# A third weight lot joins the openings by halves of a 256-token network kernel

## What is computed

```python
def first_block(x, ...):                 # two layers
    for l in range(2):
        h = rms_norm(x, ln1[l]);  x = x + mixer_block(h, ...)
        h = rms_norm(x, ln2[l]);  x = x + swiglu(h, w_ffn_in[l], w_ffn_out[l])

def second_block(x, c, ctx, ...):        # x: 256 tokens, ctx: 256 context tokens
    for layer in range(2):
        x  = x  + 0.5*mx[2]*swiglu_2(modulate(rms_norm_2(x,  g[0]), mx[0], mx[1]), ...)
        xc = xc + 0.5*mc[2]*swiglu_2(modulate(rms_norm_2(xc, g[0]), mc[0], mc[1]), ...)
        hx, hc = modulate(rms_norm_2(x, g[1]), ...), modulate(rms_norm_2(xc, g[1]), ...)
        ox, oc = (mla_mixer, swa_mixer)[layer](hx, hc, ...)
        x = x + mx[5]*ox                 # and then a second feed-forward part;
        ...                              # the context only where it is not the last layer
```

## Time and profile before

| | |
|---|---|
| times of three runs | 2615.62, 2622.36, 2624.57 us (median 2622.36) |
| the profiled execution | 2620.26 us, of which the span of its instructions is 2618.4 us |
| granted clock, mean over the span | 0.997 of full speed |
| PE busy | 2578.4 us, 98% of the span, 14982 matmuls |
| DVE busy | 1725.2 us, 66% |
| ACT busy | 1160.2 us, 44% |
| POOL busy | 39.1 us, 1% |
| read from memory | 399.10 MB |

### The profile page before, as it was taken

The page is one execution under the profiler, slowest core; times in us unless marked ns, Lnnn a source line. Parts: engine busy times, 40 slices in busy tenths (PEclk is TensorE's granted clock), DMA queues, the critical chain, the costliest instruction groups (busy, mean ns, idle before and its releaser), DMA issues.

```text
span 2618.4 us, 37370 instructions
## 1 busy us (share of the span) xinstructions
PE 2578.4 (98%) x14982; PEld 2227.8 (85%) x14982; DVE 1725.2 (66%) x2857; ACT 1160.2 (44%) x1831; POOL 39.1 (1%) x29
## 2 busy tenths in 40 slices
PE   8999999999999999999999999999999999999998
PEld 7999988999998898888887788888888888887887
DVE  6656888765678885677665565556665445576875
ACT  6565555546556552222244542222242222356553
POOL 0000000000000000000000000000000000014000
PEclk9999999999999999999999999999999999999999
DMA  5543577644456664555533024445534445342664
GB/s 192 182 153 128 178 222 218 195 137 153 138 193 202 212 191 145 161 193 179 159 127 101 1 81 149 146 145 156 165 117 145 145 142 176 125 126 65 193 207 140
DMA packets 116860, 404.56 MB, mean 155 GB/s; under 512 B 13264, under 2 KB 18512, under 8 KB 116560
## 3 DMA queue, kind: packets, MB, share of 16 engines
q1 hardware_dynamic: 116688, 402.17, 48.5%
HBM read 399.10 MB, written 1.05 MB: 153 GB/s over the span
## 4 chain that ended last, share of the span: by engine, by line
PE 91%; DVE 5%; ACT 2%; issue 1%; DMA 0%; SPq 0%; DVEq 0%; ACTq 0%
PE psum L645 21%; PE psum L647 21%; PE psum L646 21%; PE psum L651 13%; PE psum L652 6%; PE psum L1087 3%; DVE wlo L1818 1%; ACT whi L1344 1%; DVE arena L1874 1%; DVE HLO L1879 1%; PE psum L1179 1%; PE psum L1151 1%; DMA wring<-w_proj 0%; ACT HHI L1364 0%; PE psum L1169 0%
## 5 line engine op out<-in xcount | busy, mean ns | idle before, releaser
L1818 DVE TENSOR_TENSOR wlo<-wring,whi 128x1024 fp32r<-128x1024 f32 x599 | 725.6, 1223 | 307.6 <-ACT whi L1344 304.7
L1344 ACT ACTIVATE whi<-wring 128x1024 fp32r<-128x1024 f32 x599 | 622.1, 1053 | 397.9 <-PE psum L647 329.7
L645 PE MATMUL psum<-HHI,whi 128*128 128x512 f32 (+1 forms) x1448 | 532.4, 368 | 6.8 <-DVE wlo L1818 3.4
L646 PE MATMUL psum<-HLO,whi 128*128 128x512 f32 (+1 forms) x1448 | 526.5, 364 | 0.0
L647 PE MATMUL psum<-HHI,wlo 128*128 128x512 f32 (+1 forms) x1448 | 526.3, 363 | 0.0
L645 PEld LDWEIGHTS psum<-HHI,whi 128*128 128x128 f32 x1448 | 273.0, 189 | 55.2 <-DVE HLO L1879 5.8
L646 PEld LDWEIGHTS psum<-HLO,whi 128*128 128x128 f32 x1448 | 273.2, 189 | 42.7
L647 PEld LDWEIGHTS psum<-HHI,wlo 128*128 128x128 f32 x1448 | 273.1, 189 | 42.2
L645 PE MATMUL psum<-H,whi 128*128 128x256 f32 x1024 | 298.4, 291 | 8.2 <-DVE wlo L1818 4.3
L646 PE MATMUL psum<-H,whi 128*128 128x256 f32 x1024 | 290.8, 284 | 0.0
L647 PE MATMUL psum<-H,wlo 128*128 128x256 f32 x1024 | 290.7, 284 | 0.0
(11 more groups left out here) (354 smaller groups left out, 3974.2 us busy)
## 6 DMA issues: line engine op xcount, KB each, us to landing
wring<-ffn_in SPq DMA_DIRECT2D x264, 512.0 KB, 4.2
wring<-mod_w SPq DMA_DIRECT2D x144, 512.0 KB, 4.2
wring<-ffn_out SPq DMA_DIRECT2D x96, 448.0 KB, 4.0
wring<-w_proj SPq DMA_DIRECT2D x66, 512.0 KB, 3.8
wring<-w_gate SPq DMA_DIRECT2D x64, 512.0 KB, 4.1
wring<-ffn_out SPq DMA_DIRECT2D x48, 512.0 KB, 3.8
wring<-w_up SPq DMA_DIRECT2D x20, 512.0 KB, 3.5
wring<-w_out SPq DMA_DIRECT2D x16, 512.0 KB, 3.6
```

The source lines that it names most:

```text
L645: mm(out_, w[0], a[0], start=start, stop=False)
L646: mm(out_, w[0], a[1], start=False, stop=False)
L1344: A(whi[:, i % SLOTS, :], wring[:, raw_slot(tag, k), :], ACT.Copy).then_inc(sem("weights_hi"), 1)
L1818: TTN(wlo[:, i, :], wring[:, raw_slot(tag, k), :], whi[:, i, :].bitcast(F32), ALU.subtract).then_inc(sem("weights_lo"), 1)
```

## The change

The third lot (lot 2) is now multiplied in every opening by halves, as it already was in that of `("b0", 0)`. In `half_tail`, ACT converts lot 2 behind the third tile of half 0 and DVE makes its rest there, ahead of the last residual tile of half 1; lot 3 is converted behind all tiles as before. In `qkv` lot 2 is the first query lot. It is multiplied in both halves now, since `open_halves` treats all its lots alike, and the query lots done one by one begin with lot 3.

```diff
             def dense_behind(tag, norm):
-                first = 3 if norm == ("b0", 0) else 2
-                open_halves(tag, [(tag, k) for k in range(first)], norm)
-                for k in range(first, LOTS[tag]):
+                open_halves(tag, [(tag, k) for k in range(3)], norm)
+                for k in range(3, LOTS[tag]):
                     dense_lot(tag, k, BOTH, (HHI, HLO))
...
             def swa_pe():
-                open_halves("qkv", [("sq", j) for j in range(2)], ("b1", 1))
+                open_halves("qkv", [("sq", j) for j in range(3)], ("b1", 1))
...
-                query_lots(range(2, 9))
+                query_lots(range(3, 9))
...
             # ScalarE, half_tail
                 half_hi(norm, 0, range(2, 3), l, n3)
+                split_ahead(tag, lots_[1])
                 act.wait_ge(*done("x_ready", (tag, tiles_[-1])))
...
                 half_hi(norm, 1, range(KT), l, n3)
-                for k in lots_[1:]:
-                    split_ahead(tag, k)
+                split_ahead(tag, lots_[2])
...
             # VectorE, half_tail
                 s(3)
                 r(2)
+                split_ahead(tag, lots_[1])
                 for m in tiles_[:-1]:
                     add_square_half(norm, 1, m)
                 second(tiles_[-1], keys[-1])
...
                 half_norm(norm, 1, l, n3)
-                for k in lots_[1:]:
-                    split_ahead(tag, k)
+                split_ahead(tag, lots_[2])
```

## The result

The changed kernel takes 2626.51 us (median of 20 runs, 2621.1 to 2630.72), the kernel before 2621.27 (20 runs, 2615.62 to 2625.69). The ratio is 1.0018, 95% interval 1.0012 to 1.0024: slower by 4.7 us (3.1 to 6.3). The forecast was 1.1 us faster; the time lies inside the range, and inside 0.3%, but on the other side of nothing. In what follows one execution of 8431 us, of the kernel that leaves out the unread half of `qkv`, stands in that kernel's median (2623.42; 2623.2 without it) and not in its ratio.

The account below looks back on a forecast made before the run. PE was taken as the bound, holding 91% of the last-ending chain. Windows of -0.79, -1.33, -0.80 and +1.80 us (`qkv`) summed to -1.1 us, median 2622.36 to 2621.2 us; range 2615.5 to 2630.

Parts of the forecast that it names:

- The opening's work: Three lots tile by tile in each opening take PE 17.76 us where nothing is missing; waits inside and for lot 2 vanish.
- The head of the opening: PE's new wait for lot 2's rest before its first matmul makes it 1.63 us late, 1.92 in layer 0's second feed-forward.
- The signal term: From DVE's end of lot 2's conversion to PE's start at an opening: 0.03 us added.
- a fall: Granted clock at 0.50 for 3.41 us behind an idle wait of PE; priced at 1.7 us lost each time.
- `qkv`: Its opening also multiplies the context by lot 2, 2.88 us nobody reads; window 19.39 us against 17.59, +1.80.
- rival C: Later waits of PE for DVE in `qkv` swallow the +1.80 us; total -2.9, 2619.4 us; chance 0.10.
- rival B: Row swaps in `qkv` (+3 us) or late first tiles of half 1 (+1.5) are exposed: 2622.8 to 2624.2 us; chance 0.09.
- the favourable end: First tile of half 1 in the openings: about 0.6 us to spare if ACT is free, otherwise nothing.
- rival A: PE's idle 1.5 to 1.8 us at the openings lowers the clock; all four: +5.7 us, 2628.1; chance 0.20.

Follow-up runs that it names:

- the filled version: Changed kernel, but PE does 15 unused matmuls of 256 columns before waiting for lot 2 at the four openings; 2619.47 us, 0.9994 of the kernel before.

## Why the prediction was wrong

**The opening's work: right.** 17.76 us for three lots was taken from the one opening that had them, and 17.77 was measured. The waits for tiles and for lot 2 behind the opening vanished, and PE went on to lot 3 without a wait.

**The head of the opening: the mechanism right, the size too small.** The conversions came out to the hundredth (2.31 us). The signal term did not: 0.03 us, taken from DVE behind ACT, was 0.36 in PE. The fall-free windows are 19.73 to 19.75 us instead of 19.39. That is 0.35 at each of four openings, 1.4 us, and by itself it takes the forecast from -1.1 to about +0.2: the gain was gone without any fall. Against the forecast a fall costs less, 1.50 us and not 1.7, since PE's starts go from 0.12 to 0.21 us apart and not to twice the 0.12.

**`qkv`: right, and a bit dearer.** +1.80 was forecast, +2.15 measured without a fall, and the experiment that leaves the unread half out shows 2.32 us of it in the window. Nothing further on swallowed the loss (rival C): PE's waits behind the scores are 4.1 us against 4.6.

**Tight tiles and swaps (rival B): not seen.** In the changed kernel no wait for a tile or for the swapped queries is among PE's waits. The factor came early enough, since ACT was free, which the text had as the favourable end: in `qkv` ACT is idle for 1.41 us ahead of the factor, and the first tile of the second half is done at 2293.66, where PE needs it near 2294.2.

**The step that failed: the clock (rival A).** The forecast's sum set it to nothing and gave it 2 in 10. Without falls the four windows sum to -0.45 for `down`, about -1.0 for the second feed-forward (19.75 in the filled version, plus the 0.25 by which the unfilled one starts later), -0.46 and +2.15, so to about +0.2 us. Most of the measured +4.7 is the clock: over 20 runs its mean is 0.9955 against the 0.9970 of the kernel before in the later sets. One fall takes half of 3.41 us, 1.7 us, from that mean, and 0.0015 of 2622 us is 3.9, so some 2.3 falls more in a run. At 1.50 us each they cost 3.5 us, which makes +3.7 with the +0.2, inside the interval of +3.1 to +6.3. That PE's idleness brings the falls is shown, not only argued, by the wait filled with idle work: a wait nearly as long, no falls at the openings, the mean clock of the kernel before, 6 us faster.

The text set 0.66 us of idle time, which did nothing, against 2.2 us, which did, placed 1.5 to 1.8 between them and leaned to the harmless side; the missing 0.35 us then brought the idle time to 1.82 and 2.1. It also passed over a third fall in the same trace, behind a stretch of only 1.13 us near the start, where smaller waits break PE's work ahead of it as well:

```profile
27.40 0.39 PE L645 MATMUL psum<-H,whi 128*128 128x256 f32 x1 [1.13 <-DVE wlo L1818]
```

```profile
27.70:31.11 3.41, 3.41 (x18) 3.41 (x17) 3.30 (x6) 1.22 (x2) 0.00 (x0) 0.50 0.56 165
```

The page of the Trainium skill that was weighed there ("TensorE: Matmul & The Clock Gate", section "Why this matters for your kernels") spoke for no fall, and these runs show falls behind idle stretches shorter than it allows for.

**The chance.** Given an idle time between two rows of opposite outcome, the fall deserved at least an even chance at each of four openings, and a single one was enough to decide the sign.

## What to carry to other kernels

A new wait of PE costs its length, less what it saves in waits further on, and, if PE is idle in it, possibly a stretch at half clock behind it; where the trace has no idle time of that size, price both. The remedy is the order of the work: let PE begin with what is ready and join the late operand some steps later, and if there is nothing to do, even useless matmuls were cheaper here than idleness. When a helper takes on one more item, look at what it does to each: only half of what the helper did to the third lot of `qkv` was ever read.

## What the runs showed of the hardware

- **Idle time and the clock.** Over the profiles of these kernels, at the heads of the openings: no fall behind 1.04 to 1.31 us of idle time (four openings), none of three behind 1.71, 8 of 12 behind 1.81 to 1.84, and 5 of 5 behind 1.99 to 2.10. These counts are no threshold. Inside an opening, 2.32 us had none; the stretch of 2.69 us in the last stage had none in 2 of 13 profiles; the 1.13 us near the start, in the midst of smaller breaks, had one in 8 of 13. The same instruction in the same kernel had a fall in one execution and none in another. Each fall at an opening lasted 3.41 us and cost 1.5 us where PE had no slack. The spread of the times over executions tells nothing of the openings: it is 9.6 us for the changed kernel and 10.1 us for the kernel before.
- **PE behind a wait.** From the end of DVE's instruction to PE's first matmul it took 0.36 us at the head of an opening with three lots, 0.24 with two, and 0.06 inside one. With the wait filled, the window was 0.24 us shorter than the fall-free one without filling (19.49 against 19.73); its first useful matmul came 0.17 us behind DVE's end (1334.76 to 1334.93).
